# First overflow block of a mixture-of-experts layer: computed amid the expert steps, from weights loaded once into free places, in four column groups

## What is computed

```python
def hier_moe(xn, w_rg, b_rg, w_re, b_re, w_gu, w_dn):
    """Two-level routing: top-1 expert group, then top-2 experts within it; SwiGLU experts."""
    ...
    for gi in range(N_GROUPS):
        gate, up = jnp.split(jnp.einsum('nd,edf->nef', t, w_gu[gi]), 2, axis=-1)
        hmid = jax.nn.silu(gate) * up * comb[:, gi, :, None].astype(t.dtype)
        out = out + jnp.einsum('nef,efd->nd', hmid, w_dn[gi])
    return out.reshape(*lead, D_MODEL)
```

## Time and profile before

| | us |
|---|---|
| runs, median of three | 606.17 (597.13, 606.17, 606.71) |
| profiled execution, its own time | 603.64 |
| its span, first to last instruction | 601.5 |
| TensorE busy in the span | 500.5 (83%) |
| VectorE, ScalarE, GpSimd busy | 198.4, 114.4, 26.4 |
| read from memory | 127.68 MB |

### The profile page before, as it was taken

One profiled execution on the slowest core, in us unless ns is written; L12 is line 12 of the kernel. 1 busy time (PEld: TensorE's weight loads), 2 busy tenths in 40 slices (PEclk: granted clock), 3 DMA queues, 4 the chain that ended last, 5 costly groups with the idle time before them and its releaser, 6 DMA issues.

```text
span 601.5 us, 6721 instructions
## 1 busy us (share of the span) xinstructions
PE 500.5 (83%) x2616; PEld 282.6 (47%) x2616; DVE 198.4 (33%) x566; ACT 114.4 (19%) x242; POOL 26.4 (4%) x52
## 2 busy tenths in 40 slices
PE   0799999999996999997599985969696979577780
PEld 0665555655665667664575432424242524116220
DVE  1100001243535345263527440506060614042234
ACT  5321012111111525234311010101010101000004
POOL 4000021000005010001000000000000000000000
PEclk9989999999996799899589997979797989676775
DMA  8996060000019412002509999999999999914002
GB/s 268 383 387 185 17 211 35 2 0 1 0 34 416 163 35 71 19 1 74 243 10 408 412 422 412 421 413 422 412 422 410 422 412 423 411 54 195 0 0 105
DMA packets 37654, 131.31 MB, mean 218 GB/s; under 512 B 10162, under 2 KB 10198, under 8 KB 29304
## 3 DMA queue, kind: packets, MB, share of 16 engines
q1 hardware_dynamic: 36440, 127.17, 54.0%
q10 hardware_dynamic: 576, 2.10, 0.9%
q0 software_dynamic: 608, 1.62, 0.7%
HBM read 127.68 MB, written 3.19 MB: 218 GB/s over the span
## 4 chain that ended last, share of the span: by engine, by line
PE 63%; DMA 24%; DVE 6%; ACT 3%; SPq 2%; issue 1%; DVEq 0%; ACTq 0%
PE bank L1298 59%; DMA gu_ring<-in_w_expert_gate_up 23%; SPq L483 1%; DMA X<-in_x 1%; PE bank L1486 1%; PE bank L1405 1%; PE bank L1327 1%; PE bank L1456 1%; DVE X L1286 1%; DVE r_xs L892 1%; ACT r_xT L847 1%; DVE pnorm L952 0%; ACT r_xT L652 0%; DVE r_qz L1038 0%; DVE r_kT L1192 0%
## 5 line engine op out<-in xcount | busy, mean ns | idle before, releaser
L1298 PE MATMUL bank<-gu_ring,r_xT 128*32 128x512 f32 (+1 forms) x576 | 101.9, 704 | 31.9 <-DMA gu_ring<-in_w_expert_gate_up 31.9
L1298 PEld LDWEIGHTS bank<-gu_ring,r_xT 128*32 128x32 f32 (+1 forms) x576 | 30.9, 133 | 99.5 <-issue 99.5
L1298 PE MATMUL bank<-r_xT,gu_ring 128*128 128x384 f32 x192 | 64.4, 496 | 0.0
L1298 PE MATMUL bank<-BT,r_qz 128*128 128x128 f32 (+1 forms) x432 | 56.8, 296 | 8.1 <-DVE BT L1143 4.2
L1298 PEld LDWEIGHTS bank<-BT,r_qz 128*128 128x128 f32 x432 | 55.2, 212 | 15.0 <-issue 10.4
L1298 PE MATMUL bank<-r_xs 128*128 128x512 f32 (+1 forms) x108 | 53.7, 629 | 0.9 <-ACT r_xs L843 0.9
L1298 PEld LDWEIGHTS bank<-r_xT,gu_ring 128*128 128x128 f32 x192 | 37.1, 195 | 25.0 <-issue 1.4
L1298 PE MATMUL bank<-dn_ring,V 128*32 128x512 f32 x264 | 37.3, 644 | 6.9 <-ACT V L806 4.2
L1298 PE MATMUL bank<-r_xT,dn_ring 128*128 128x384 f32 x128 | 42.6, 486 | 0.0
L1220 DVE TENSOR_TENSOR X<-X,bank 128x512 f32<-128x512 f32 x48 | 33.0, 687 | 12.9 <-PE bank L1298 12.2
L1190 DVE TENSOR_SCALAR r_kT<-r_kT 128x256 f32<-128x256 f32 x8 | 2.4, 294 | 101.1 <-ACT r_kT L796 101.1
(11 more groups left out here) (264 smaller groups left out, 507.8 us busy)
## 6 DMA issues: line engine op xcount, KB each, us to landing
gu_ring<-in_w_expert_gate_up SPq DMA_DIRECT2D x64, 1024.0 KB, 18.5
dn_ring<-in_w_expert_down SPq DMA_DIRECT2D x33, 1024.0 KB, 18.8
gu_ring<-in_w_in SPq DMA_DIRECT2D x4, 2048.0 KB, 13.4
dn_ring<-in_w_in SPq DMA_DIRECT2D x2, 2048.0 KB, 19.4
gu_ring<-in_w_out SPq DMA_DIRECT2D x2, 2048.0 KB, 8.9
r_xs<-in_cache_k SPq DMA_DIRECT2D x8, 256.0 KB, 8.7
r_xs<-in_cache_v SPq DMA_DIRECT2D x8, 256.0 KB, 6.8
gu_ring<-in_w_expert_gate_up SPq DMA_DIRECT2D x1, 2048.0 KB, 7.9
```

The lines of the kernel that those rows point to most:

```text
L1298: return te.matmul(out, lhsT, rhs, start=start, stop=stop, **kw)
```

## The change

The first overflow block is taken out of the loop and computed in steps 1 to 4 by instructions of its own, whether or not there is such a block.

- Its weights are loaded by six transfers (`load_spare`), issued by SyncE behind the down loads of quad 1, into tiles that the attention phase used: oB, oT, r_kc, parts of r_xs, r_pr. The expert comes from a register; with no block it is the last expert. 3.15 MB.
- Step 1: `spare_select` builds the selection, `spare_gather` gathers rows and block weights. Step 2: `spare_up` computes gate and up, with the hidden columns dealt over four column groups (128 result columns each), and the turned selection; `spare_swiglu` follows. Step 3: `spare_turn` transposes, `spare_down` computes down with 256 columns in each column group, `spare_rows` scales. Step 4: `combine` adds to each of its six products a second one, of the block.
- The count of blocks for the loop after step 7 is one less, not below 0, and the loop reads expert and base one entry later.
- GpSimd sets the block's result rows to zero once (128x1024).

The diff, without the new semaphores:

```diff
--- before.py
+++ after.py
@@ -50,6 +50,7 @@
 HALF_K = KT // 2
 FAR = 1.0e6
 RING = 4
+AT_GATHER, AT_UP, AT_DOWN, AT_ADD = 1, 2, 3, 4
 MAXOV = PAIRS // SLOTS
 OVROWS = 16 * -(-(MAXOV + 1) // 16)
 CONSTS = 20
@@ -142,6 +143,21 @@
         slot_no = r_U[:, D:D + P]
         tmpc = sb("tmpc", [P, NTOK])
+        oB_flat = oB[:, :, :].rearrange("p c t -> p (c t)")
+        oT_flat = oT[:, :, :].rearrange("p c t -> p (c t)")
+        spare_gu = [oB_flat[:, 512 * i:512 * (i + 1)] for i in range(3)]
+        spare_gu += [oT_flat[:, 512 * i:512 * (i + 1)] for i in range(3)]
+        spare_gu += [r_kc[:, i, :] for i in range(2)]
+        free_xs = D + 4 * NTOK
+        spare_dn = [r_xs[:, free_xs + 512 * i:free_xs + 512 * (i + 1)] for i in range(3)] + [r_pr[:, :]]
+        sp_pickT = tmpc
+        sp_xgT = pnorm[0][:, 0:KT * SLOTS].rearrange("p (k s) -> p k s", k=KT)
+        sp_y = oB_flat[:, 0:D]
+        sp_pick = pT[0][:, 0:TT * SLOTS].rearrange("p (t s) -> p t s", t=TT)
+        sp_w = pT[0][:, 2 * P - 1:2 * P]
+        sp_glu = pT[1][:, 0:P]
+        sp_hT = pT[1][:, P:P + FT * SLOTS].rearrange("p (j s) -> p j s", j=FT)
         gbc = r_U[:, 0:D]
         ident = sb("ident", [P, P])
@@ -485,6 +516,17 @@
             def load_down(n, h):
                 sp.dma_start(dn_ring[:, h, :].rearrange("p (j n) -> p j n", j=FT), w_dn[n * WIDE + h]).then_inc(ld_dn[h], 16)
+            def load_spare():
+                sp.wait_ge(ovr_regs, 1)
+                e = sp.value_load(ov_regs[0:1, 0:1], min_val=0, max_val=E - 1)
+                sp.dma_start(oB_flat, w_gu[e][:, 0:3 * 512]).then_inc(sp_ld, 16)
+                sp.dma_start(oT_flat, w_gu[e][:, 3 * 512:6 * 512]).then_inc(sp_ld, 16)
+                sp.dma_start(r_kc[:, :, :].rearrange("p i n -> p (i n)"), w_gu[e][:, 6 * 512:8 * 512]).then_inc(sp_ld, 16)
+                sp.dma_start(r_xs[:, free_xs:free_xs + D], w_dn[e][:, 0, :]).then_inc(sp_ld, 16)
+                sp.dma_start(spare_dn[2], w_dn[e][:, 1, 0:512]).then_inc(sp_ld, 16)
+                sp.dma_start(spare_dn[3], w_dn[e][:, 1, 512:D]).then_inc(sp_ld, 16)
             sp.wait_ge(g_full, g_of["B", CT - 1] + 1)
             for half in range(2):
                 for h in (2, 3):
@@ -514,15 +556,16 @@
                 sp.wait_ge(y_full, n)
                 for h in range(WIDE):
                     load_down(n, h)
-            sp.wait_ge(ovr_regs, 1)
+                if n == 1:
+                    load_spare()
             sp.wait_ge(y_full, QUADS)
             n_ov = sp.value_load(ov_regs[0:1, 2 * OVROWS:2 * OVROWS + 1], min_val=0, max_val=MAXOV)
             with sp.If(n_ov > 0):
                 with sp.Fori(0, n_ov) as i:
                     sp.wait_ge(y_full, i + QUADS)
-                    e = sp.value_load(ov_regs[0:1, bass.ds(i, 1)], min_val=0, max_val=E - 1)
+                    e = sp.value_load(ov_regs[0:1, 1:OVROWS][:, bass.ds(i, 1)], min_val=0, max_val=E - 1)
                     sp.dma_start(gu_ring[:, 0, :], w_gu[e]).then_inc(ov_w, 16)
                     sp.dma_start(dn_ring[:, 0, :].rearrange("p (j n) -> p j n", j=FT), w_dn[e]).then_inc(ov_w, 16)
@@ -617,6 +660,9 @@
             g.iota(slot_no, [[1, P]], base=0, channel_multiplier=0, allow_small_or_imprecise_dtypes=True).then_inc(slot_no_done, 1)
             gains_a(2)
+            pool.wait_ge(sp_gu_full, 1)
+            g.memset(sp_y, 0.0).then_inc(sp_y_zero, 1)
             pool.wait_ge(t_evac, T_LAST + 1)
             pool.dma_start(o["conv_p"], last_row[0:2, :]).then_inc(st_out, 16)
             pool.dma_start(o["conv_s"], last_row[2:2 + 2 * NB, :]).then_inc(st_out, 16)
@@ -811,6 +857,19 @@
                     act.wait_ge(c_full, 2 * TT * n)
                 s.activation(y_rows[:, 0:512], bO[0][:, :], ACT.Copy, scale=w_all[:, n:n + 1]).then_inc(y_evac_a, 1)
+                if n == AT_GATHER:
+                    act.wait_ge(sp_w_evac, 1)
+                    s.activation(sp_xgT, bS[0][:, 256:512].rearrange("p (k s) -> p k s", k=KT), ACT.Copy).then_inc(sp_xg_evac, 1)
+                if n == AT_UP:
+                    act.wait_ge(sp_gu_full, 1)
+                    s.activation(sp_glu[:, 0:64], bS[0][:, 0:64], ACT.Exp, scale=-1.0).then_inc(sp_gexp, 1)
+                    s.activation(sp_pickT[:, :], bS[0][:, P:P + NTOK], ACT.Copy).then_inc(sp_pickT_evac, 1)
+                if n == AT_DOWN:
+                    act.wait_ge(sp_ht_full, 1)
+                    for up in range(2):
+                        rows = slice(64 * up, 64 * up + 64)
+                        src = bS[0][rows, 0:P].rearrange("p (j g s) -> p j g s", j=FT, g=2)[:, :, up, :]
+                        s.activation(sp_hT[rows, :, :], src, ACT.Copy).then_inc(sp_ht_evac, 1)
                 if n + 1 < QUADS:
                     gate_exp(n + 1)
@@ -1175,7 +1234,8 @@
                 link(v.tensor_tensor(ovr[:, 3:4], tok_id[:, 0:1], ovr[:, 3:4], ALU.subtract))
                 link(v.tensor_scalar(ovr[:, 3:4], ovr[:, 3:4], 1.0, float(SLOTS), ALU.add, ALU.mult))
                 link(v.scalar_tensor_tensor(ovr[:, 1:2], ovr[:, 0:1], float(LIST), ovr[:, 3:4], ALU.mult, ALU.add))
-                v.tensor_copy(ovr[:, 2:3], ovi[:, E - 1:E]).then_inc(ovr_done, 1)
+                link(v.tensor_scalar(ovr[:, 2:3], ovi[:, E - 1:E], -1.0, 0.0, ALU.add, ALU.max))
+                v.tensor_scalar(ovr[:, 0:1], ovr[:, 0:1], float(E - 1), None, ALU.min).then_inc(ovr_done, 1)
             def overflow_regs():
@@ -1219,7 +1279,47 @@
                     dve.wait_ge(c_full, j + 1)
                     v.tensor_tensor(X[:, t, cs], X[:, t, cs], bC[j % 2][:, :], ALU.add).then_inc(c_evac, 1)
+            def spare_select():
+                for c in range(2):
+                    for t in range(TT):
+                        ins = v.tensor_scalar(ranked[:, c, t, :], slot_no[:, 0:SLOTS], ov_base[:, 0:1],
+                                              okey[:, c, t:t + 1], ALU.add, ALU.is_equal)
+                ins.then_inc(sp_c, 1)
+                dve.wait_ge(sp_c, 1)
+                v.tensor_tensor(sp_pick, ranked[:, 0, :, :], ranked[:, 1, :, :], ALU.add).then_inc(sp_sel, 1)
+            def spare_weight():
+                dve.wait_ge(sp_xg_full, 1)
+                v.tensor_copy(sp_w, bS[0][:, 0:1]).then_inc(sp_w_evac, 1)
+            def spare_swiglu():
+                gl, bank = sp_glu, bS[0]
+                dve.wait_ge(sp_gexp, 1)
+                dve.wait_ge(sp_pickT_evac, 1)
+                v.tensor_scalar_add(gl[:, 0:64], gl[:, 0:64], 1.0).then_inc(sp_c, 1)
+                dve.wait_ge(sp_c, 2)
+                v.reciprocal(gl[:, 0:64], gl[:, 0:64]).then_inc(sp_c, 1)
+                dve.wait_ge(sp_c, 3)
+                v.tensor_tensor(gl[:, 0:64], gl[:, 0:64], bank[:, 0:64], ALU.mult).then_inc(sp_c, 1)
+                dve.wait_ge(sp_c, 4)
+                v.tensor_tensor(gl[:, 64:128], gl[:, 0:64], bank[:, 64:128], ALU.mult).then_inc(sp_glu_done, 1)
+            def spare_rows():
+                dve.wait_ge(sp_y_full, 1)
+                dve.wait_ge(sp_w_evac, 1)
+                dve.wait_ge(sp_y_zero, 1)
+                for g in range(WIDE):
+                    rows = slice(g * SLOTS, (g + 1) * SLOTS)
+                    ins = v.tensor_scalar(sp_y[rows, g * 256:(g + 1) * 256], bS[0][rows, 256:512], sp_w[rows, :], None, ALU.mult)
+                ins.then_inc(sp_y_evac, 1)
             def step(n):
+                if n == AT_GATHER:
+                    spare_select()
                 if n + 2 < QUADS:
                     pick_step(n + 2)
                 turned(n)
@@ -1230,7 +1330,13 @@
                 v.tensor_scalar(y_rows[:, 512:D], bO[1][:, :], w_all[:, n:n + 1], None, ALU.mult).then_inc(y_evac_d, 1)
                 if n == 0:
                     overflow_regs()
+                if n == AT_GATHER:
+                    spare_weight()
                 add_rows(n)
+                if n == AT_UP:
+                    spare_swiglu()
+                if n == AT_DOWN:
+                    spare_rows()
                 if n + 1 < QUADS:
                     swiglu(n + 1)
@@ -1245,7 +1351,7 @@
             n_ov = dve.value_load(ov_regs[0:1, 2 * OVROWS:2 * OVROWS + 1], min_val=0, max_val=MAXOV)
             with dve.If(n_ov > 0):
                 with dve.Fori(0, n_ov) as i:
-                    v.tensor_copy(base_now[:, :], ov_base[:, bass.ds(i, 1)]).then_inc(ov_base_set, 1)
+                    v.tensor_copy(base_now[:, :], ov_base[:, 1:OVROWS][:, bass.ds(i, 1)]).then_inc(ov_base_set, 1)
                     dve.wait_ge(ov_base_set, i + 1)
                     for c in range(2):
                         for t in range(TT):
@@ -1547,6 +1653,14 @@
                     pe.wait_ge(ovr_regs, 1)
                 if n >= 1:
                     pe.wait_ge(ht_evac, n)
+                if n == AT_GATHER + 1:
+                    pe.wait_ge(sp_xg_evac, 1)
+                    pe.wait_ge(sp_w_evac, 1)
+                if n == AT_UP + 1:
+                    pe.wait_ge(sp_pickT_evac, 1)
```

(68 more changed lines are left out.)

## The result

| | us |
|---|---|
| changed kernel, median of four runs | 569.95 (568.52 to 570.33) |
| kernel before, median of four runs | 605.97 (597.13 to 606.71) |
| ratio | 0.9472, 95% interval 0.9353 to 0.9591 |
| profiled execution of the changed kernel, span | 569.95, 567.7 |

What follows compares the result with a forecast made beforehand. Bound: the stream of expert weights, then a chain on one overflow block. Span 601.50 - 43.26 + 2.07 + 7.60 = 567.91, plus 2.14 outside the span, gives 570.1 us; range 562 to 578, own range 565 to 576 at 0.84.

Steps and rivals of the forecast that it cites:

- The pass at the end: After step 7, the overflow block's single loop pass goes: 43.26 us removed, from 544.07 to 587.33.
- What is kept: After step 7: count load and branch 0.99, jump 1.0, hand to ScalarE 0.08; 2.07 us given back.
- the jump over the body: After step 7, the branch now taken past the loop's code: 1.0 us, between 0 and 1.7.
- The stream: Six transfers behind step 1's down weights move every later landing by 7.60 us; bounds 0 and 11.9.
- The last addition: End of step 7: everything behind the last gu_ring wait moves 7.60 us; squares start 2 us after it, near 553.7.
- The last wait: Step 7's wait for gu_ring, before quad 7's second half, ends near 528 us instead of 520.4.
- TensorE's added work: Block's products in steps 1 to 4: 17.2 us, at most 37, held by waits for gu_ring, so costing 0.
- The lead: At quad 4's loads: TensorE may free a place some 14.9 us later before the weight loads run dry.
- The slow-clock rival: TensorE stays at its lower clock level through the steps: at 1.2 GHz 88 us more, 658; chance 0.01.

Runs made afterwards that it cites:

- traces of three: Changed kernel with step 1's gather and weight products done three times over, same results: 578.28 us, ratio 0.9569 to the kernel before.
- six times: Changed kernel with step 1's gather and weight products done six times over, same results: 613.85 us, ratio 1.0148 to the kernel before.

## Why the prediction was right, point by point

- *The pass at the end.* Right. 43.26 us by the profile of before, confirmed with it alone taken away: 42.7, where 43.26 less the 1.21 that stays would be 42.05. What is kept was 1.21 us and not 2.07: the jump over the body took 0.22 where I took 1.0 between 0 and 1.7. By the Trainium skill (Runtime: NRT & Kernel Launch, Instruction fetch mechanics) a target outside the two pages held makes a wait. No such wait shows in the traces of the changed kernel and of the one with the pass taken away, which both skip the body; whether their targets lay inside those pages is not shown.
- *The stream.* Right in kind and near in size: 7.60 forecast for the transfers; 7.50 and 7.73 by leaving them out, by the profiles, and 7.6 and 8.5 by medians. The 7.97 between the first two profiles is 7.73 of the transfers and 1.57 of the work, less the 1.33 by which the trace of before is longer than the later one of the same steps: that it came so near 7.60 is in part luck. The Trainium skill (DMA: Bandwidth & Descriptors, Anatomy of one DMA) gives a fixed 2.0 us for each transfer issued from GpSimd. These six were issued by SyncE into a full queue, and nothing like it shows: they cost 7.5 to 7.7, against the 19.2 of that estimate.
- *Where the sum closed by luck.* The last addition moved from 543.37 to 551.63, 8.26 and not 7.60. That is 2.27 of a later start of the stream, 7.97 of the stream, and 1.98 given back: quad 7's second half took 4.96 us where it took 6.46, step 7's down product 4.97 where it took 6.01, less 0.8 of a longer wait ahead of that (1.29 for its weights, where there were 0.47 for ScalarE). The last wait ended at 530.61, not near 528, mainly by the late start. The first issue for quad 1 lies between 312.24 (without the transfers) and 317.25 (the changed kernel again) in the profiles of the variants, with the same code ahead of it, so it is scatter. The 0.66 over and the 0.86 less that was kept cancel: this is luck.
- *TensorE's added work.* The total was near, 17.2 forecast and 17.4 measured, with terms that were off both ways. The block's products took 6.67, 2.52, 1.25 (0.36 and 0.89) and 4.7 (10.50 less 5.8), 15.1 together, and there are 2.25 that I had not seen: step 1's combination took 8.11 us and not 5.86, since the clock had fallen behind the gather (granted 0.70 in 360 to 370 us). That the work costs nothing was right to within 2 us.
- *The lead.* The step that was wrong, though nothing hung on it here: "TensorE may free a place some 14.9 us later than it does before the stream runs dry". By the same reckoning the changed kernel has 378.48 + 10.1 - 372.75 = 15.8; the runs show 12 to 13. I took the turn of a load as the moment at which it may be issued at the latest, and reckoned that turn from the wait that ends last. The traces of three and six times size both parts. The DMA engines had moved all that was issued by 384.1 and 384.4 us, counting what they moved at 416 GB/s, where my reckoning gives 386.0 and 386.3: 1.9 us too late. And a load issued to the empty queue needs time: behind quad 3's first issue in the trace of six, 425.93, they moved 66, 188, 295 and 401 GB/s in the four microseconds from 426, which is 1.8 us less than a full stream moves, as much as in the trace of three. 15.8 less 3.7 is 12.1. It did not matter here: one gather delays nothing, as quad 3's loads are issued at 372.75, and at 374.15 in the kernel without the work.
- *The slow-clock rival.* It did not come, and its price for whole steps was never tested. Its argument held in part: with shorter waits gate_up ran 6.3 us faster. But I had missed that the gather's own kind of product lets the clock fall with no wait at all, as in the six repeats at 0.50. One gather is too short for that to matter; six made the kernel 1.5% slower than the one before (1.0148), by the price of the repeats at the low clock and the lead. It was not the rival's mechanism even there: from 430 to 470 us the granted clock was 1.00 again.

## What to carry to other kernels

Work moved from a serial tail into a stage bound by a stream costs what its bytes take in the stream, and its instructions are free, or nearly so, as long as two budgets hold: the waits for the stream, and the lead of the loads over their turn. Read the lead from the issues, and take some 4 us off it, as here: the stream had run dry 1.9 us before the reckoned turn, and lost 1.8 us when it started again. Where the clock is low behind waits, work put into them gives some of its time back. Then look for idle stretches of the DMA engines ahead of the stream: free places are worth more if they are filled there.

## What was not expected of the hardware

Products with 32 moving columns and 128x128 weights, back to back and with TensorE busy throughout, ran at granted clock 0.50, 10.45 us for 48 records; with 128 moving columns, and another moving operand, they ran at 1.00, 27.07 us for 240. A busy engine was not enough to keep 2.4 GHz. And skipping VectorE's whole loop body cost 0.22 us.
